# Expert rows of the second layer weighed at eviction and added to the output by accumulating transfers

## The reference, cut to what matters

```python
def run_block(args):
    xb, e = args
    return (jax.nn.silu(xb @ w1[e]) * (xb @ w3[e])) @ w2[e]
ys = lax.map(run_block, (xs, block_e)).reshape(n_slots, D)
return jnp.einsum("tkd,tk->td", ys[dest].reshape(T, TOP_K, D), w)
...
y = hier_moe(tokens, ...)              # tokens = modulate(x, norm_ffn, mod[3], mod[4])
x = x + mod[5] * y                     # after the second layer x is the output
```

## Time and profile before

| | |
|---|---|
| median of 3 runs | 2343.88 us (2340.59 to 2344.8) |
| profiled execution's span | 2340.7 us, mean granted TensorE clock 0.964 |
| PE (matmuls) busy | 2160.9 us, 92% |
| DVE, ACT, POOL busy | 970.1, 765.2, 178.3 us |
| moved by DMA | 601.00 MB, mean 257 GB/s |
| L2038 + L2075, both layers | 498.2 + 247.2 us of PE |

### The profile page before, as it was taken

How to read it: one execution, slowest core, us unless ns; L and a number is a source line. 1 busy time by engine, 2 the same in 40 slices (tenths; PEclk the granted TensorE clock), 3 DMA queues, 4 the chain that set the end, 5 groups by cost and what they waited for, 6 DMA issues and landing times. The chain is left out here.

```text
span 2340.7 us, 33433 instructions
## 1 busy us (share of the span) xinstructions
PE 2160.9 (92%) x14090; PEld 1203.8 (51%) x14090; DVE 970.1 (41%) x1477; ACT 765.2 (33%) x1154; POOL 178.3 (8%) x126
## 2 busy tenths in 40 slices
PE   7999989989997999999999789898989999998875
PEld 5788876546663555555555344445843333332222
DVE  6333326656235445444454454666462111111113
ACT  5411005544133434444344256564231010100001
POOL 0010000000000000000000303550000000000002
PEclk9999999999998999999999999999999999999987
DMA  9201117026629999999999801001158999999996
GB/s 355 59 28 37 37 46 322 1 82 243 225 79 348 425 419 427 427 426 424 427 427 385 276 10 36 27 10 36 36 192 367 425 419 413 422 426 426 426 427 247
DMA packets 147673, 601.00 MB, mean 257 GB/s; under 512 B 25060, under 2 KB 61632, under 8 KB 122560
## 3 DMA queue, kind: packets, MB, share of 16 engines
q1 hardware_dynamic: 117824, 520.67, 55.4%
q0 software_dynamic: 11952, 43.52, 4.8%
q10 hardware_dynamic: 17744, 34.62, 4.0%
HBM read 537.43 MB, written 61.34 MB: 256 GB/s over the span
## 5 line engine op out<-in xcount | busy, mean ns | idle before, releaser
L2038 PE MATMUL ph<-w,x_t 128*32 128x512 f32 x4352 | 498.2, 611 | 33.3 <-DMA w<-in_exp_w 32.2
L2038 PEld LDWEIGHTS ph<-w,x_t 128*32 128x32 f32 x4352 | 142.1, 112 | 334.7 <-issue 330.5
L2273 DVE TENSOR_TENSOR hidden<-hidden,ph 64x512 f32<-64x512 f32 x68 | 73.8, 1085 | 441.7 <-ACT hidden L2191 440.8
L2075 PE MATMUL py<-w,g_t 128*32 128x512 f32 x2176 | 247.2, 594 | 2.4 <-DVE g_t L2283 1.3
L2191 ACT ACTIVATE hidden<-ph 64x512 f32<-64x512 f32 x68 | 40.2, 591 | 570.1 <-PE ph L2038 570.1
L2264 DVE TENSOR_TENSOR w_low<-w,w_high 128x1024 fp32r<-128x1024 f32 x156 | 180.5, 1219 | 13.0 <-ACT w_high L2177 12.8
L2548 PE MATMUL z<-hT,w_cd 128*128 128x512 f32 (+1 forms) x448 | 183.5, 566 | 0.0
L1624 POOL DMA_INDIRECT x_rows<-h_tokens,index x47 | 44.4, 945 | 1668.2 <-PE px L2022 926.8
L806 PE MATMUL z<-h_high,w_hi 128*128 128x512 f32 (+1 forms) x432 | 159.6, 370 | 3.9 <-DVE h_low L901 3.5
L2177 ACT ACTIVATE w_high<-w 128x1024 fp32r<-128x1024 f32 x156 | 152.1, 1048 | 19.5 <-PE ph L2048 15.5
L807 PE MATMUL z<-h_low,w_hi 128*128 128x512 f32 (+1 forms) x432 | 155.7, 360 | 0.0
(11 more groups left out here) (372 smaller groups left out, 2979.8 us busy)
## 6 DMA issues: line engine op xcount, KB each, us to landing
w<-in_exp_w SPq DMA_DIRECT2D x192, 2048.0 KB, 23.5
ada_raw<-in_ada_w SPq DMA_DIRECT2D x13, 2048.0 KB, 8.9
y_slots<-y_rows ACTq DMA_DIRECT2D x136, 128.0 KB, 9.7
w<-in_ada_w SPq DMA_DIRECT2D x8, 2048.0 KB, 13.6
y_slots<-zero SPq DMA_DIRECT2D x29, 512.0 KB, 15.0
h_tokens<-h_rows ACTq DMA_DIRECT2D x18, 512.0 KB, 4.4
w_ab<-in_w_in_ab SPq DMA_DIRECT2D x14, 512.0 KB
y_slots<-y_rows ACTq DMA_DIRECT2D x26, 256.0 KB
```

The costliest lines, as they stand in the source:

```text
L2038: ins = pe.matmul(ph[row:row + UNIT, :], xt[:, k, at:at + UNIT], w13[place[u + n] % RING][:, half, k, :], start=(k == 0), stop=(k == KT - 1))
L2075: ins = pe.matmul(py[bufs[i][0]][row:row + UNIT, :], gt[:, k, n * UNIT:(n + 1) * UNIT], w2[place[u + n] % RING][:, k, half * 512:(half + 1 ...
L2273: dve.tensor_tensor(hid[PAIR:P, :].rearrange("s (k q) -> s q k", k=FT), hid[0:PAIR, :].rearrange("s (q k) -> s q k", k=FT), ph[PAIR:P, :]. ...
```

## The change

`last_rows` and, for the second layer, the stores to `y_slots` go. `route` of the second layer turns `xT` back into rows and stores them in `out`; a second pair of products of one-hot matrices (`rows_of_slots`) gives for each slot its row of `out` seen as 2048 half rows of 512 (`to_row`; a slot without a token gets a number past the end) and its weight (`slot_w`). In `experts` VectorE's eviction multiplies by the gate and by the slot's weight, and GpSimd adds the result to `out` by indirect transfers that accumulate, skipping rows past the end. A transfer waits for the one before. An item whose two units belong to different experts takes two transfers, one per unit (`adds_of`). The loop for the rest builds its weighted sum on TensorE and adds it to `out` on VectorE (not shown; it does not run here). One clearing of semaphores moves from before `layer_odd` to behind it.

```diff
@@ -279,10 +283,9 @@
             self.first_layer()
             self.clear_semaphores()
             self.feed_forward(0, NT)
+            self.layer_odd()
             self.clear_semaphores()
-            self.layer_odd()
             self.feed_forward(1, LT)
-            self.last_rows()
 
 
     def first_layer(self):
...
@@ -1717,6 +1734,38 @@
                         pe.matmul(bc[w * UNIT:(w + 1) * UNIT, 512:512 + NU // 4], op[:, c, t, :], ou[:, c, t, w::4],
                                   start=(n == 0), stop=(n == len(pairs) - 1))
                 pe.transpose(bc[:, 1024:1024 + P], rcol[:].to_broadcast([P, P]), self.c("ident")).then_inc(s_index, 1)
+
+            def first_rows_pe(pe, n):
+                if n < 2:
+                    pe.wait_ge(s_rank, 1)
+                else:
+                    pe.wait_ge(s_xe, n - 1)
+                for k in range(4):
+                    ins = pe.transpose((tr[0], ssum)[n % 2][:, k * P:(k + 1) * P], self.xT[:, 4 * (n % 2) + k, (n // 2) * P:(n // 2 + 1) * P],
+                                       self.c("ident"))
+                ins.then_inc(s_xp, 1)
+
+            def first_rows_act(act, t):
+                for n in (2 * t, 2 * t + 1):
+                    act.wait_ge(s_xp, n + 1)
+                    if n % 2 == 0:
+                        if t < HROWS:
+                            act.wait_ge(s_hw[t], 16 * len(range(t, nt, HROWS)))
+                        else:
+                            act.wait_ge(s_first[t % HROWS], 16 * (t // HROWS))
+                    act.activation(hrows[:, t % HROWS, (n % 2) * 512:(n % 2 + 1) * 512], (tr[0], ssum)[n % 2][:], ACT.Copy).then_inc(s_xe, 1)
+                act.wait_ge(s_xe, 2 * t + 2)
+                act.dma_start(self.out[0, t * P:(t + 1) * P, :], hrows[:, t % HROWS, :]).then_inc(s_first[t % HROWS], 16)
+
+            def rows_of_slots(pe):
+                pe.wait_ge(s_weigh, 1)
+                pairs = [(c, t) for c in range(2) for t in range(nt)]
+                for out, at_place in ((pcnt, op), (pr, ow)):
+                    for n, (c, t) in enumerate(pairs):
+                        for w in range(4):
+                            ins = pe.matmul(out[w * UNIT:(w + 1) * UNIT, 0:NI], at_place[:, c, t, :], ou[:, c, t, w % 2::2],
+                                            start=(n == 0), stop=(n == len(pairs) - 1))
+                ins.then_inc(s_rows, 1)
 
             @block.scalar
             def _(act):
...
@@ -1741,6 +1790,9 @@
                         act.dma_start(self.h[t * P:(t + 1) * P, :], hrows[:, t % HROWS, :]).then_inc(s_hw[t % HROWS], 16)
                 exps(act)
                 self.ada_row_out(act, ada, 0)
+                if closing:
+                    for t in range(nt):
+                        first_rows_act(act, t)
 
             @block.tensor
             def _(pe):
@@ -1779,11 +1831,20 @@
                 for h in range(len(ADA_BEHIND), NA):
                     self.ada_pe(pe, ada, h)
                 pe.wait_ge(s_te, 2 * nt)
-                self.keep_running(pe, tr[0][:], max(0, 7 - 4 * max(0, NA - len(ADA_BEHIND))))
+                if closing:
+                    for n in range(FIRST_BEFORE):
+                        first_rows_pe(pe, n)
+                else:
+                    self.keep_running(pe, tr[0][:], max(0, 7 - 4 * max(0, NA - len(ADA_BEHIND))))
                 pe.wait_ge(ada["row_out"], 1)
                 indices(pe)
                 self.ada_turn(pe, ada, 0)
-                self.keep_running(pe, tr[0][:], 4)
+                if closing:
+                    for n in range(FIRST_BEFORE, 2 * nt):
+                        first_rows_pe(pe, n)
+                    rows_of_slots(pe)
+                else:
+                    self.keep_running(pe, tr[0][:], 4)
 
             @block.gpsimd
             def _(pool):
@@ -1900,7 +1961,20 @@
                 dve.wait_ge(s_index, 1)
                 dve.tensor_copy(self.index[:, 0:NU // 4], bc[:, 512:512 + NU // 4]).then_inc(s_table, 1)
                 do(dve.tensor_copy(self.table[:, TAB_REST:TAB_REST + 64], bc[0:1, 1024:1024 + 64]))
+                if closing:
+                    do(dve.tensor_tensor(ow[:], every(self.c("count", UNIT), UNIT), wide(partf[:, 1, :, :], UNIT), ALU.is_equal))
+                    do(dve.tensor_tensor(op[:], op[:], ow[:], ALU.add))
+                    dve.tensor_tensor(ow[:], ow[:], wide(self.wgt[:, :, 0:nt], UNIT), ALU.mult).then_inc(s_weigh, 1)
                 self.ada_finish(dve, ada, 0)
+                if closing:
+                    dve.wait_ge(s_rows, 1)
+                    do(dve.tensor_scalar(rowf[:, 3, :], pcnt[:, 0:NI], 0.0, NO_ROW, ALU.is_equal, ALU.mult))
+                    do(dve.scalar_tensor_tensor(rowf[:, 3, :], pcnt[:, 0:NI], 2.0, rowf[:, 3, :], ALU.mult, ALU.add))
+                    do(dve.tensor_scalar(rowf[:, 0, :], rowf[:, 3, :], self.c("row_half", 1), None, ALU.add))
+                    do(dve.tensor_scalar(rowf[:, 1, :], rowf[:, 0, :], self.c("row_unit", 1), None, ALU.add))
+                    do(dve.tensor_scalar(rowf[:, 2, :], rowf[:, 0, :], self.c("row_unit", 1), NO_ROW, ALU.subtract, ALU.add))
+                    do(dve.tensor_copy(to_row[:], rowf[:, 0:3, :]))
+                    do(dve.tensor_copy(slot_w[:], pr[:, 0:NI]))
 
     def experts(self, layer, nt, ring):
 
...
+                adds_of = [[0] if place[u] == place[u + n - 1] else [1, 2] for q, u, n in items]
+                added_by = [sum(len(a) for a in adds_of[0:i + 1]) for i in range(N)]
...
@@ -1991,6 +2077,8 @@
                     sp.dma_start(self.xT[:, 0:KT // 2, :], self.xs[:, 0:KT // 2, :]).then_inc(s_back, 16)
 
                 sp.wait_ge(s_b, N)
+                if gated:
+                    sp.wait_ge(s_add, 16 * added_by[-1])
 
                 def body(b):
                     e = sp.value_load(self.table[0:1, bass.ds(TAB_REST + b, 1)], min_val=0, max_val=NE - 1)
...
@@ -2010,9 +2107,32 @@
 
             @block.gpsimd
             def _(pool):
-                for q in range(1, NQUAD):
+                def gather(q):
                     pool.wait_ge(s_tx, q)
                     self.gather_rows(pool, ring, q)
+
+                def add_rows(i):
+                    pool.wait_ge(s_ye, i + 1)
+                    for n, which in enumerate(adds_of[i]):
+                        before = added_by[i] - len(adds_of[i]) + n
+                        if before:
+                            pool.wait_ge(s_add, 16 * before)
+                        pool.indirect_dma_start(out_rows, bass.IndirectOffsetOnAxis(to_row[:, which, i:i + 1], 0), yr[:, bufs[i][0], :], None,
+                                                bounds_check=2 * SEQ - 1, oob_is_err=False, compute_op=ALU.add).then_inc(s_add, 16)
+
+                if gated:
+                    gather(1)
+                    for i in range(N):
+                        if i + 1 < N and ends_quad[i + 1] and items[i + 1][0] + 2 < NQUAD:
+                            gather(items[i + 1][0] + 2)
+                        if i == 0:
+                            for n in range(HROWS):
+                                pool.wait_ge(s_first[n], 16 * len(range(n, nt, HROWS)))
+                        add_rows(i)
+                    pool.wait_ge(s_add, 16 * added_by[-1])
+                else:
+                    for q in range(1, NQUAD):
+                        gather(q)
 
             @block.tensor
             def _(pe):
...
@@ -2219,10 +2352,13 @@
                             x_out(items[i + 1][0] + 1)
                     if i + 2 < N and full[i + 2]:
                         high(i + 2, range(0, HI_RING))
-                    if i >= 0:
+                    if i >= 0 and not gated:
                         y_out(i)
-                for u in range(2):
-                    act.wait_ge(s_st[u], filled[u])
+                if gated:
+                    act.wait_ge(s_add, 16 * added_by[-1])
+                else:
+                    for u in range(2):
+                        act.wait_ge(s_st[u], filled[u])
 
                 def body(b):
                     act.wait_ge(v_tx, b + 1)
...
@@ -2284,11 +2420,11 @@
 
                 def y_gated(i):
                     dve.wait_ge(s_b, i + 1)
-                    for half, buf in zip((0, 1), sorted(bufs[i])):
-                        if done_before[i][buf]:
-                            dve.wait_ge(s_st[buf], done_before[i][buf])
-                        dve.tensor_tensor(in_two(yr[:, buf, :]), in_two(py[buf][:]), gate_half[half] if full[i] else gate_pair,
-                                          ALU.mult).then_inc(s_ye, 1)
+                    buf = bufs[i][0]
+                    if i >= 2:
+                        dve.wait_ge(s_add, 16 * added_by[i - 2])
+                    dve.scalar_tensor_tensor(in_two(yr[:, buf, :]), in_two(py[buf][:]), slot_w[:, i:i + 1], gate_pair,
+                                             ALU.mult, ALU.mult).then_inc(s_ye, 1)
 
                 if gated:
```

(23 more changed lines are left out.)

120 lines of the change are left out of this document (57 added, 63 removed).

## The result

The changed kernel takes 2357.25 us (median of 4 runs, 2355.9 to 2360.03), the kernel before on the same chip 2344.34 us (2340.59 to 2347.17): ratio 1.0066, 95% interval 1.0049 to 1.0083. It is slower, by 13 us or 0.7%. The forecast was 2330 us and faster; the time is inside the whole range, and the sign is that of rivals 2 and 3.

What follows compares the result with a forecast made beforehand. TensorE's pace, then the weight stream, bound the kernel before; the transfer chain would take over: 1796.7 + 523.5 + 6 = 2326.2, span about 2327, median 3.2 us above, so 2330 us. Range for 8 in 10: 2306 to 2405.

Steps and rivals of the forecast that it cites:

- Rival 2: Expert stage: reading, adding and writing back makes a transfer dearer than a gather; slower, 2360 us; chance 0.23.
- rival 3: Expert stage: empty places take packets, so no step is short; span 2392 us, 2367 with half given back; chance 0.17.
- if places outside the bounds make no packet: 8.9 us: Expert-stage chain: a half-filled transfer saves 3.4 us of 12.3; 19 steps at 8.9 us make 169.1 us.
- the other limit: Expert stage: TensorE and the weights, rather than the chain, would end the span at 2309 us.
- Route part: Before the expert stage: added work makes the experts start 6 us later (0 to 12), with nothing given back downstream.
- Removal of the old stores: Expert stage: 84 stores to `y_slots`, 10.49 MB, listed as removed, with no time in the sum.
- chain stays hidden: Expert stage: loaded transfers under 11 us, so TensorE and the weights set the end; 2312 us; chance 0.18.
- A full step: Expert-stage chain: one loaded transfer takes 12.0 + 0.3 = 12.3 us, as a gather does; 28 of them, 344.4 us.
- the 6 us for gathers ahead: Expert-stage chain: transfers issued behind a gather on GpSimd's queue wait a little, 20 times 0.3 us.
- The end: After the last product: the last two transfers take 5 us each, then about 1 us to the span's end.
- A pile of four or more transfers: Behind the last product: a pile of four at 5 us would take 20 us of the closing 44.7.
- The marks: Signs named for trace: 49 transfers landing in 11 to 13 us, split ones about 9, first expert product at 1775.

## Why the prediction was wrong

**Which step failed.** The forecast's sum goes along the chain, and its step "if places outside the bounds make no packet: 8.9 us" failed. The 14 steps of split transfers took 10.9 us in the mean, together 28 us more than the sum had; 28 us on the forecast span of 2327 give 2355, and the span is 2354.0. That the other errors nearly cancel is luck: the sum further down has them. Beside this the other limit was wrong too, by traffic that the prediction left without a term; with it hardly a gain is left even with a hidden chain.

**Route part: the place right, the size wrong.** Predicted +6 us (0 to 12), measured +12.4 (and +13.4 alone). Ahead of the index matmuls it was 6.5 where I took 4; behind them 5.9 where I took 2. The second step failed most: four groups and 256 small instructions were priced by the busy times of the earlier trace rows, where they stand in a burst of 128, without the gap of 2.6 us that the longer burst has. By luck R came 4.3 us earlier in the traced execution, so the first result was only 2.1 us late in place of 6.4.

**Removal of the old stores: priced at nothing, worth 10.2 us.** I listed them as removed and gave them no term, although showed the DMA engines at 0.99 to 1.01. And TensorE's 28.6 us of waits for weights were the place where such traffic shows.

**The transfers' traffic: the missing term, about 28 us.** The prediction treated a transfer as a wait only, and took the other limit as before's last product plus the late start: 2309. With two chains that limit could be seen, and it came to 2336.1: 2.5 us more for S (7.7 more from R, less 5.2 by which R came earlier), 18.1 in the stage and 6.8 at the end. Rival 2 had the mechanism, reading, adding and writing back beside a saturated queue, but priced it as latency of the chain alone. With this term the case "chain stays hidden" is a span of 2336 and not 2309, runs of 2338 and not 2312, and the forecast has hardly a path to a gain.

**Chain: the loaded step right, the half-filled step wrong.** A full step was taken at 12.3 us; the 32 steps behind unsplit transfers have a median of 12.5. A half-filled one was taken at 8.9, because an engine with 4 rows in place of 8 would save 3.4 us; the 14 behind split transfers have a median of 11.6. Places outside the bounds do make packets: 44 transfers and 19 gathers between 1780 and 2300 us make 9091 packets on their queue, 63 x 144 = 9072. That is rival 3's mechanism, with the time given back where the weights let up that the prediction named: by all steps together (2337.39 - 1799.81) / 47 = 11.4 us. From the first result to the last landing it took 549.1 us (1798.85 to 2347.95), where I had 529.5. Of the 19.6 us more, the split steps make +28.2 (152.8 against 14 x 8.9), the others with the last three -3.6, the 6 us for gathers ahead that weren't needed -6.0, and the time from the first result to the first transfer +1.0. Against the stage's own limit, traffic included, the chain is 16 us longer.

**The end.** The rows of after:

```profile
2337.39 1.55 POOL L2120 DMA_INDIRECT out<-y_rows,to_row  x1 [4.03 <-DMA out<-y_rows,to_row]
...
2343.06 1.55 POOL L2120 DMA_INDIRECT out<-y_rows,to_row  x1 [4.12 <-DMA out<-y_rows,to_row]
2347.95 0.06 DVE L2458 MEMSET y_rows<- 128x1 f32 x1 [9.00 <-DMA out<-y_rows,to_row]
```

The last transfers step in 5.7 and 4.9 us, as predicted (5.0). But from the last landing to the span's end it is 6.0 us, where I took 1 us; with no transfers at all it is 5.6 us from the last product. In the kernel before it is at most 0.4 us: its last store is issued at 2337.5 us, these stores land after 2.8 us at the least, and the span is 2340.7. What fills the 6.0 us is open. A pile of four or more transfers did not form, since VectorE lets only two be open.

**The sum, corrected.** The first result's end came 2.1 us later than predicted (1798.85 against 1796.7), the chain from there 19.6 us longer, the end 5.0: 2327.2 + 26.7 = 2353.9, against a span of 2354.0.

**The marks** named ahead held for the transfers (49, landing 11.5 us) and VectorE's waits (17 of 42 items, not most); the first expert product started at 1777.06 us (1775 named), and in the first half the results come every 12.0 us instead of 11.4; the split transfers did not land in 9 us; the last landing came 9.9 us behind the last product, not 20 to 30. "In sign if the split transfers take as long as whole ones" held.

No version that does all the work is faster than the kernel before. The chain's 16 us came back in three ways, and each ends at 2338 to 2339 us, within 0.2% of before; of the three only the small weight packets leave the output whole. The closing stage's 28.8 us (31 with two chains) then pays for 12.4 to 13.7 us of route part and 18.1 of traffic.

## What to carry to other kernels

Where the DMA engines are near 1.0, every transfer is a term by its engine time as well as by its latency, removed ones included: take the queues' share over their bytes, and for a read-modify-write twice a store's. For a chain of dependent transfers multiply the number of transfers, not of rows, by the loaded latency, and look where one item needs two steps. Work moved ahead of a saturated stage costs its full length if the stage's stream starts behind it; price it by its stores' landings, not by its busy times.

## What the runs showed of the hardware that was not expected

- An accumulating indirect transfer of 128 rows of 2 KB takes GpSimd 1.55 us to generate (0.99 as a plain scatter), lands in 3.6 us at the least, 11.5 in the median beside packets of 16 KB and 9.0 beside packets of 8 KB. Its engine time per MB is 86 us against 43 for plain stores. A plain scatter of the same rows makes 82 packets, the accumulating one 144.
- Places outside the bounds make packets that wait their turn: 144 packets, 0.05 MB, 11.4 us.
- A long burst of small matmuls (256 instructions of 42 columns) has gaps of 0.5 to 5.5 us that the profile puts to issue. Each ends 2.2 to 2.6 us behind the start of a 16 KB packet on the instruction queue (3.2 to 3.5 where the packet takes twice as long); that this is the cause is not shown. Why the part ahead of R differs by up to 16 us between the traced executions is open.
